# Second block's entry: squares summed with tokens on partitions, the root on four columns, spread to a bank; borders set behind the feed

## What is computed

```python
x = layer_norm(ALPHA * x + m[:, 5] * conv_glu_ffn(...), post_ln_g[l, 1], post_ln_b[l, 1])   # end of the first block

def _rmsnorm(x, g):
    xf = x.astype(jnp.float32)
    y = xf * lax.rsqrt(jnp.mean(xf * xf, axis=-1, keepdims=True) + NORM_EPS)
    return (y * g.astype(jnp.float32)).astype(x.dtype)

def second_block(x, attn_norm, w_in, ...):
    h = _rmsnorm(x, attn_norm[l])
    proj = h @ w_in[l]
    p_nsa, p_rw, p_moba = _split_2(proj, [N_IN_NSA, N_IN_RWKV, N_IN_MOBA])
    ...
```

## Time and profile before

| | us |
|---|---|
| median of 3 runs | 2927.93 |
| lowest, highest | 2926.86, 2928.55 |
| the profiled execution, its own time | 2931.61 |
| its span | 2929.8 |
| TensorE busy in the span | 2674.3 (91%), 16244 records |
| VectorE busy | 1645.7 (56%) |
| ScalarE busy | 1090.3 (37%) |
| mean granted clock of TensorE | 0.955 of 2.4 GHz |
| entry, first VectorE instruction to the end of the reciprocal | 2082.83 to 2101.44 |
| first feed step of `projections` | 2103.63 |
| first matmul of `projections` | 2105.69 |

### The profile page before, as it was taken

How to read it: one execution, slowest core, us unless ns; L and a number is a source line. 1 busy time by engine, 2 the same in 40 slices (tenths; PEclk the granted TensorE clock), 3 DMA queues, 4 the chain that set the end, 5 groups by cost and what they waited for, 6 DMA issues and landing times. The chain is left out here.

```text
span 2929.8 us, 41986 instructions
## 1 busy us (share of the span) xinstructions
PE 2674.3 (91%) x16244; PEld 2078.7 (71%) x16244; DVE 1645.7 (56%) x2659; ACT 1090.3 (37%) x1787; POOL 72.7 (2%) x89
## 2 busy tenths in 40 slices
PE   6978899965598999999998899999899999999998
PEld 3743688754487778878654578878678877788886
DVE  3526412267724478864599678864555566554432
ACT  3431110136434265532432465532321154355521
POOL 0015200000000000000000000000000000000000
PEclk9989999996699999999999899999999999999999
DMA  8723312200024233332111233342152000333232
GB/s 299 250 95 136 115 51 64 58 2 2 17 70 125 65 94 97 96 108 79 44 44 29 57 87 93 100 110 84 50 131 70 3 2 16 82 106 99 86 104 68
DMA packets 381859, 240.93 MB, mean 82 GB/s; under 512 B 7568, under 2 KB 353552, under 8 KB 381712
## 3 DMA queue, kind: packets, MB, share of 16 engines
q1 hardware_dynamic: 381712, 238.89, 27.7%
HBM read 236.24 MB, written 2.10 MB: 81 GB/s over the span
## 5 line engine op out<-in xcount | busy, mean ns | idle before, releaser
L1085 DVE SCALAR_TENSOR_TENSOR ffn_acc<-ffn_pad,cols_sb,ffn_acc 128x512 f32<-128x512 f32 x380 | 264.0, 749 | 32.6 <-ACT ffn_acc L1012 32.6
L223 PE MATMUL bank<-ffn_x_high,pre_high 128*128 128x512 f32 x528 | 210.8, 399 | 4.8 <-DVE ffn_x_low L452 3.3
L225 PE MATMUL bank<-ffn_x_high,pre_low 128*128 128x512 f32 x528 | 209.0, 396 | 0.0
L224 PE MATMUL bank<-ffn_x_low,pre_high 128*128 128x512 f32 x528 | 208.9, 396 | 0.0
L225 PE MATMUL bank<-ffn_x_high,ffn_w_low 128*128 128x512 f32 x528 | 205.5, 389 | 0.0
L223 PE MATMUL bank<-ffn_x_high,ffn_w_high 128*128 128x512 f32 x528 | 205.5, 389 | 0.0
L224 PE MATMUL bank<-ffn_x_low,ffn_w_high 128*128 128x512 f32 x528 | 205.4, 389 | 0.0
L223 PE MATMUL bank<-ffn_h_high,ffn_down_w_high 128*128 128x512 f32 x480 | 190.5, 397 | 0.7 <-DVE ffn_h_low L880 0.7
L224 PE MATMUL bank<-ffn_h_low,ffn_down_w_high 128*128 128x512 f32 x480 | 189.6, 395 | 0.0
L225 PE MATMUL bank<-ffn_h_high,ffn_down_w_low 128*128 128x512 f32 x480 | 188.6, 393 | 0.0
L685 ACT ACTIVATE ffn_down_w_high<-ffn_down_ring 128x1408 fp32r<-128x1408 f32 (+1 forms) x45 | 60.5, 1344 | 210.9 <-PE bank L225 179.4
(11 more groups left out here) (711 smaller groups left out, 6198.0 us busy)
## 6 DMA issues: line engine op xcount, KB each, us to landing
ada_ring<-in_ada_w SPq DMA_DIRECT2D x48, 1024.0 KB, 7.1
pre_ring<-in_ffn_w_up SPq DMA_DIRECT2D x88, 512.0 KB, 3.9
pre_ring<-in_ffn_w_in SPq DMA_DIRECT2D x44, 512.0 KB, 3.9
ffn_down_ring<-in_ffn_w_down SPq DMA_DIRECT2D x28, 704.0 KB, 4.4
pj_ring<-in_w_in SPq DMA_DIRECT2D x24, 512.0 KB, 3.9
ffn_down_ring<-in_ffn_w_out SPq DMA_DIRECT2D x14, 704.0 KB, 4.4
pre_ring<-in_conf_w SPq DMA_DIRECT2D x18, 512.0 KB, 4.8
f_ring<-in_mix_w_in SPq DMA_DIRECT2D x32, 256.0 KB, 3.0
```

What stands on the lines that cost most here:

```text
L223: pe.matmul(bank, weights[0], acts[0], start=start, stop=False)
L224: pe.matmul(bank, weights[0], acts[1], start=False, stop=False)
L225: return pe.matmul(bank, weights[1], acts[0], start=False, stop=stop)
L1085: dve.scalar_tensor_tensor(out=dst, in0=src, scalar=conv_w(2 * i + j, n), in1=dst, op0=ALU.mult, op1=ALU.add).then_inc(tapped[j], 1)
```

## The change

In `second_entry` the sum of squares is taken with tokens on partitions: for each tile four matmuls of one column instead of one of 512 columns, each into a column of its own in bank 5 (32 columns in all, nothing accumulated). VectorE adds the eight columns of each token group (`tensor_reduce` to 128x4), forms the mean plus epsilon, ScalarE takes the root, VectorE the reciprocal, all on 128x4 in `se_stat`. Four matmuls spread the result to bank 5, as `spread_tokens` does, and the feed reads it from there instead of `core.rstd`. The fills behind the sums are 1 ahead of the spread and 2 behind it, instead of 5. ScalarE takes the root of a column of ones, `se_one`, ahead of the real one, and VectorE sets this column at the stage's start. In `projections` the six memsets stand behind the feed.

```diff
--- before.py
+++ after.py
@@ -1375,14 +1375,15 @@
 
 
 
-    with core.room(se_sq=[P, 2, SEQ]) as (sq,):
-        with core.stage("scaled", "centered", "formed_x", "squared", "summed", "var_done", "root_done") as (
-                block, scaled, centered, formed_x, squared, summed, var_done, root_done):
+    with core.room(se_sq=[P, 2, SEQ], se_stat=[P, 3, TT], se_one=[P, 1]) as (sq, stat, one):
+        with core.stage("scaled", "centered", "formed_x", "squared", "summed", "added", "var_done", "root_done", "inverted", "one_in") as (
+                block, scaled, centered, formed_x, squared, summed, added, var_done, root_done, inverted, one_in):
             squares = core.banks[5]
             rstd, mean = core.banks[6], core.banks[7]
 
             @block.vector
             def _(dve):
+                dve.memset(one[:, :], 1.0).then_inc(one_in, 1)
                 for k in range(DT):
                     dve.tensor_tensor(x[:, k, :], x[:, k, :], rstd[:, :], ALU.mult).then_inc(scaled, 1)
                     if k:
@@ -1391,9 +1392,11 @@
                 dve.wait_ge(scaled, DT)
                 dve.tensor_tensor(x[:, DT - 1, :], x[:, DT - 1, :], mean[:, :], ALU.add).then_inc(centered, 1)
                 dve.wait_ge(summed, DT)
-                dve.tensor_scalar(core.rstd[:, :], squares[:, :], 1.0 / D, NORM_EPS, ALU.mult, ALU.add).then_inc(var_done, 1)
+                dve.tensor_reduce(stat[:, 0, :], squares[:, 0:DT * TT].rearrange("p (k b) -> p b k", b=TT), AX_X, ALU.add).then_inc(added, 1)
+                dve.wait_ge(added, 1)
+                dve.tensor_scalar(stat[:, 1, :], stat[:, 0, :], 1.0 / D, NORM_EPS, ALU.mult, ALU.add).then_inc(var_done, 1)
                 dve.wait_ge(root_done, 1)
-                dve.reciprocal(core.rstd[:, :], core.rstd[:, :])
+                dve.reciprocal(stat[:, 2, :], stat[:, 1, :]).then_inc(inverted, 1)
 
             def square(act, k):
                 act.wait_ge(formed_x, k + 1)
@@ -1409,17 +1412,26 @@
                     if k:
                         square(act, k - 1)
                 square(act, DT - 1)
+                act.wait_ge(one_in, 1)
+                act.activation(one[:, :], one[:, :], ACT.Sqrt)
                 act.wait_ge(var_done, 1)
-                act.activation(core.rstd[:, :], core.rstd[:, :], ACT.Sqrt).then_inc(root_done, 1)
+                act.activation(stat[:, 1, :], stat[:, 1, :], ACT.Sqrt).then_inc(root_done, 1)
 
             @block.tensor
             def _(pe):
                 fill(pe, core, core.banks[4], 3)
                 for k in range(DT):
                     pe.wait_ge(squared, k + 1)
-                    pe.matmul(squares[:, :], core.const("ones"), sq[:, k % 2, :], start=(k == 0), stop=(k == DT - 1))\
-                      .then_inc(summed, 1)
-                fill(pe, core, core.banks[4], 5)
+                    for b in range(TT):
+                        mm = pe.matmul(squares[:, k * TT + b:k * TT + b + 1], sq[:, k % 2, b * P:(b + 1) * P], core.const("ones")[:, 0:1],
+                                       start=True, stop=True)
+                    mm.then_inc(summed, 1)
+                fill(pe, core, core.banks[4], 1)
+                pe.wait_ge(inverted, 1)
+                for b in range(TT):
+                    pe.matmul(core.banks[5][:, b * P:(b + 1) * P], stat[:, 2, b:b + 1].broadcast_to([P, P]), core.const("ident"),
+                              start=True, stop=True)
+                fill(pe, core, core.banks[4], 2)
 
 
 def final_norm(core, x, gain, out):
@@ -3260,7 +3272,7 @@
     wide = w.rearrange("(k p) f -> p k f", p=P)
     kilo = 1024
     t2 = core.in_arena("pj_t2", [P, 2, SEQ], F32, 0)
-    feed = RootFeed(core, entering, h, t2, root_gain, core.rstd[:, :])
+    feed = RootFeed(core, entering, h, t2, root_gain, banks[5][:, :])
     reset = core.in_arena("pj_reset", [P, 2 * SEQ], F32, 4 * kilo)
     x = core.in_arena("pj_x", [P, 2, pairs, KV_H, N_CMP], F32, 8 * kilo)
     third = core.in_arena("pj_w1", [P, pairs, P], F32, 16 * kilo)
@@ -3701,6 +3713,7 @@
                 if s == 25:
                     weigh()
 
+            feed.dve(dve, formed, fed_high, fed)
             for n in range(2):
                 dve.memset(raw[n][:, 0:1], 0.0).then_inc(cleared, 1)
             dve.memset(reset[:, :], 1.0).then_inc(cleared, 1)
@@ -3708,7 +3721,6 @@
             dve.memset(reset[:, ::RW_C], 0.0).then_inc(cleared, 1)
             dve.memset(out.kc[:], 0.0).then_inc(cleared, 1)
             dve.memset(out.vc[:], 0.0).then_inc(cleared, 1)
-            feed.dve(dve, formed, fed_high, fed)
             for s in range(PREPARED, SLABS):
                 n = s - PREPARED
                 dve.wait_ge(slab_in[slot(s)], 16 * (n // SLOTS + 1))
```

## The result

The changed kernel takes 2932.99 us in the median of 20 runs (2930.24 to 2937.60); the kernel before, run beside it, 2928.70 us in the median of 20 (2926.26 to 2933.12). The ratio is 1.0014 with a 95% interval of 1.0008 to 1.0021: slower by 4.1 us (2.3 to 6.1). That is less than the 0.2% that the prediction took for the limit of what can be measured, yet the interval leaves out 1, so the slowdown is clear of the scatter. The median lies 0.2 us above the forecast's own range. The profiled execution took 2936.27 us around a span of 2934.5, before 2931.61 around 2929.8; the mean granted clock was 0.953 (before 0.955).

A forecast was written before the change was run, and what follows sets the result against it. Bound: the second_entry chain in which nothing else runs, then TensorE from the block's first matmul. Terms summed to +3.4, pulled to +3.3 us: 2931.2 us; own range 2928.8 to 2932.8, 8 in 10 range 2925.4 to 2932.8.

The forecast's parts named there:

- Rival A: Entry sums: the clock stays high because loading weights counts as work; -1.9 to -2.6 us, 2925.9 us; chance 0.15.
- rival B: Entry sums: the clock falls but one-column records keep their 0.115 us; -0.2 us, 2927.7 us; chance 0.08.
- Memset +0.05: Start of second_entry: a one-column memset opens VectorE's list, on which the entry waits; +0.05 us (0 to 0.1).
- Sums +3.6 (3.0 to 4.2): Sums in second_entry: the clock falls in the first or second tile, then 1.74 us per tile; +3.6 us.
- Behind the sums +0.9: From sums to last fills: 5.7 us against 4.78, the clock returning during the last fills; +0.9 us (-0.83 to +2.2).
- Stage end +0.25: End of second_entry: led by TensorE, it takes 1.05 us against 0.77; +0.25 us (0.1 to 0.3).
- Memsets -1.42: Start of projections: memsets moved behind the feed let it start earlier, covered before the slab's split; -1.42 us.
- the term 0 for the feed's low clock: Feed's first matmuls: the present loss stays, seven matmuls at 0.43 instead of 0.23 us, 1.4 us; change 0.
- Rival C: Feed in first_tiles: the clock stays low for 20 more matmuls; +4.0 us on top, +7.3, 2935.2 us; chance 0.05.
- Rival D: Behind the sums: fills eat the shorter root, 0.83 of 3.72 us left at full clock; in the sum, no separate chance.

The follow-up runs named there:

- e3_wide: Changed kernel with the sums' 32 matmuls over 128 columns of ones, accumulated over tiles, and no reduce; 2928.44 us, ratio 0.9995 to the kernel before.
- e9_changed_fill: Changed kernel with three more fills at the next stage's start, ahead of the block's first matmul; 2933.69 us, ratio 1.0013 to the kernel before.
- e4_no_fill: Changed kernel without the two fills behind the spread; 2932.48 us, ratio 1.0014 to the kernel before.
- e1_borders: Kernel before with only the six memsets moved behind the feed; 2929.17 us, ratio 0.9997 to the kernel before.
- e8_changed_again: Changed kernel measured once more, unaltered, beside the others on one chip; 2933.97 us, ratio 1.0017 to the kernel before.
- e2_sums: Changed kernel with the six memsets put back ahead of the feed; 2935.32 us, ratio 1.0022 to the kernel before.
- e5_fill_feed: Kernel before with three more fills at the next stage's start, ahead of the block's first matmul; 2928.31 us, ratio 0.9996 to the kernel before.

## Why the prediction was right and wrong

**The direction and the mechanism of the sums** were right: slower, because the clock falls in the one-column sums. e3_wide shows it: with the same loads beside 128 columns the clock stays and the 4 us do not come up. That the difference could hardly be told from none was too cautious: 20 runs of each kernel did tell it. Rival A (the clock stays high) and rival B (low clock, records keep their price) fell: eight records took 1.71 us at 0.50, where the spread's row had given 1.74. The page "TensorE: Matmul & The Clock Gate" of the Trainium skill, section "LDWEIGHTS (loading the stationary operand)", has the load's time as its columns over 1.2 GHz, with no second figure for the low clock; for 128 columns that is some 107 ns, an estimate from the page's rule. Here a load measured 186 to 192 ns at 1.00 and 333 ns at 0.50. By that rule the sums would not have slowed down; the measurement decides against it.

**The terms of the sum.** Memset +0.05: nothing, VectorE's first multiply stands at the same 2080.73. Sums +3.6 (3.0 to 4.2): +4.00; the fall came in the first of the two tiles that were named, and the sums ended at 17.83 us, which is 2100.66 in the times of the earlier trace rows, where 2100.6 was forecast. Behind the sums +0.9: +1.14; 5.92 us instead of the 5.7 taken. Stage end +0.25: -0.02; the meeting behind TensorE's last fill took 0.75 us, not the 1.05 of the earlier trace rows. Memsets -1.42: -1.42, covered, since the split of the slab ended at 2118.88 and TensorE took it at 2121.05. Sum of these, forecast +3.38, measured +3.70 at the feed's first step. One addition of the prediction is off by 0.02 us (1.06 + 1.0 + 1.72 + 0.15 is 3.93, not 3.95), which changes nothing.

**The step that failed** is "so I keep the loss that the gap of 4.7 us brings now (seven matmuls at 0.43 instead of 0.23, 1.4 us)", the term 0 for the feed's low clock. It took the low stretch of the kernel before over as it was. It was 14 matmuls instead of seven, and from the first feed step to the slab 15.82 us instead of 14.29: +1.53 (0.13 of it for the feed's slower read of the bank). e9_changed_fill shows it on the chip: take the low clock out of the feed and 2.1 us of that stretch go. Rival C thus came in part: by the prediction's own sign, a low clock past ten matmuls, this is C, with seven matmuls more and not the 20 that it named. Its reason against, that TensorE is never idle at the low level and now comes back after seven, was no bound on how long the level lasts; the earlier trace rows showed 8.9 us of it and should have been in the sum as a range of 0 to +1.5 at least, not of -0.67 to +0.3. Why the stretch was the longer one in the changed kernel stays open (see the last section).

**The size of the whole.** Up to the slab the change costs 5.23 us where +3.3 was forecast. Of the difference of 1.9, 1.4 to 1.5 are that step, 0.4 the sums, 0.24 the work behind them, and -0.27 the stage end. The medians show less, +4.3 (ratio 4.1, and 5.0 in the repetition): the rest is in the scatter ahead of the entry and behind the slab, which no step of the sum had. Beside it the median of before moved from 2927.93 (3 runs) to 2928.70 (20 runs), 0.77 us. That alone is more than the 0.2 us by which the range was missed, so whether the time came out just inside or just outside of it was luck; the term of the feed was wrong by 1.5 us either way. The range was too narrow: its upper end, 2932.8, held the forecast's own terms and nothing for the base nor for a part of C.

**Rival D**, the fills eating the shorter root, was rightly in the sum. At the low clock it is larger than at the full one: the two fills cost 2.3 us (e4_no_fill) where 1.72 had been taken, and with the slow spread nothing was left of the shorter root.

## What to carry to other kernels

A sum over partitions by one-column matmuls looks like the cheapest form, and its weight loads fill TensorE in the profile, but in a row of eight such tiles it ran at half the clock in all five executions; the same loads beside 128 columns cost nothing more and kept it in all four. A fill belongs into the time in which TensorE would idle anyway (ahead of the feed's first matmul), not ahead of a stage's end, where it is on the path of all engines. When a low-clock stretch can follow a gap, put its double length into the range, and take the base's own scatter in as well.

## What the runs showed of the hardware

The low stretch of the feed had one of two lengths. It lasted 3.4 us, seven to nine matmuls, in four executions (before, e1_borders, e3_wide, e4_no_fill) and 6.8 us in three: 14 matmuls in after and e8_changed_again, 11 in e2_sums. In the short ones the first matmul came at most 0.3 us behind the fall (in e1_borders ahead of it), in the long ones 0.8 us (after, e8_changed_again) and 2.1 us (e2_sums) behind it. The three long ones have the one-column sums with the two fills behind the spread in common, and a low stretch ahead of the entry, which the profile of before had too, with a short one in the feed. What decides between the lengths was not tried apart, so the runs show what the long stretch costs, but not why the changed kernel met it.

The wide sums of the kernel before are not safe either: with the entry's code unchanged the clock fell in them in e1_borders (6.3 to 9.7) and e5_fill_feed (6.1 to 9.5), and the sums ended 0.44 and 0.59 us later than in the profile of before. In that profile, as in after, e2_sums and e8_changed_again, a low stretch lay ahead of the entry (-4.8 to -1.4) that these two, and the other executions, did not have. With it the one-column sums lost the clock at 5.4 or 5.5, without it at 6.5.
